# Idle products on TensorE taken out of the mixer stage of a two-layer encoder step

## What is computed

```python
p = rmsnorm(x, P['norm_mix']) @ P['w_in']
p_rg, p_gate, p_rw, p_mla = jnp.split(p, MIX_SPLITS, axis=-1)
y_rg, ... = rglru_mixer(p_rg, p_gate, rg_buf, rg_h, P)
y_rw, ... = rwkv7_mixer(p_rw, rw_shift, rw_state, P)      # delta-rule recurrence, 4 heads x 64
q_lat, q_rope, ckv, kr = mla_project(p_mla, pos, P)       # attention, 8 heads
y = jnp.concatenate([y_rg, y_rw, y_mla], axis=-1) @ P['w_out']
x = x + y
x = x + mem_attend(rmsnorm(x, P['norm_mem']), ...)
x = x + jnp.square(jax.nn.relu(rmsnorm(x, P['norm_ffn']) @ P['ffn_w1'])) @ P['ffn_w2']
```

## Time and profile before

| | us |
|---|---|
| median of 3 runs | 1875.14 (1874.27 to 1875.53) |
| the profiled execution | 1873.22 |
| its span in the trace | 1871.4 |
| TensorE matmul busy (records may overlap) | 1783.0, 95% |
| VectorE busy | 1143.1, 61% |
| ScalarE busy | 868.0, 46% |

### The profile page before, as it was taken

One profiled execution on the slowest core, in us unless ns is written; L12 is line 12 of the kernel. 1 busy time (PEld: TensorE's weight loads), 2 busy tenths in 40 slices (PEclk: granted clock), 3 DMA queues, 4 the chain that ended last, 5 costly groups with the idle time before them and its releaser, 6 DMA issues.

```text
span 1871.4 us, 38137 instructions
## 1 busy us (share of the span) xinstructions
PE 1783.0 (95%) x16290; PEld 1650.4 (88%) x16290; DVE 1143.1 (61%) x1977; ACT 868.0 (46%) x1588; POOL 259.5 (14%) x222
## 2 busy tenths in 40 slices
PE   5998988999999999999999999989999999999997
PEld 5985776899889999999999667769987999999996
DVE  6678666454457765666467776655444786556653
ACT  5444546453356544444345355554534664444432
POOL 2020000200013222221100100002000232222201
PEclk9999999999999999999999999999999999999998
DMA  6200001453012222222231000123610222222221
GB/s 225 68 20 1 4 3 48 147 172 133 35 57 80 102 95 99 91 91 95 88 127 57 9 1 4 37 94 122 214 57 13 101 79 102 93 95 96 91 92 59
DMA packets 38760, 149.56 MB, mean 80 GB/s; under 512 B 4416, under 2 KB 4576, under 8 KB 36928
## 3 DMA queue, kind: packets, MB, share of 16 engines
q1 hardware_dynamic: 36288, 131.05, 20.6%
q0 software_dynamic: 2304, 16.06, 2.3%
HBM read 139.68 MB, written 7.41 MB: 79 GB/s over the span
## 4 chain that ended last, share of the span: by engine, by line
PE 79%; DVE 10%; ACT 7%; issue 2%; POOL 1%; DMA 1%; DVEq 0%; ACTq 0%; SPq 0%; POOLq 0%
PE PS L816 58%; PE PS L979 13%; PE PS L1008 5%; PE PS L998 2%; DVE wL L1885 1%; DVE wL L1889 1%; ACT wH L1402 1%; DVE hbL L2358 1%; PE PS L1256 1%; ACT hb L1402 1%; ACT L1402 1%; DVE xT L1915 1%; DVE stat L2250 1%; POOL sq L707 1%; ACT sq L1402 0%
## 5 line engine op out<-in xcount | busy, mean ns | idle before, releaser
L1402 ACT ACTIVATE wH<-ring 128x1024 fp32r<-128x1024 f32 (+1 forms) x294 | 261.6, 891 | 327.6 <-PE PS L816 266.7
L816 PE MATMUL PS<-hH,wH 128*128 128x272 f32 x1760 | 384.4, 300 | 29.6 <-DVE hL L1898 19.0
L816 PE MATMUL PS<-hH,wL 128*128 128x272 f32 x1760 | 367.6, 290 | 0.0
L816 PE MATMUL PS<-hL,wH 128*128 128x272 f32 x1760 | 366.9, 290 | 0.0
L1889 DVE TENSOR_TENSOR wL<-ring,wH 128x1024 fp32r<-128x1024 f32 x182 | 230.9, 1270 | 188.1 <-ACT wH L1402 187.4
L816 PEld LDWEIGHTS PS<-hH,wH 128*128 128x128 f32 x1760 | 279.9, 190 | 46.1 <-issue 17.8
L816 PEld LDWEIGHTS PS<-hH,wL 128*128 128x128 f32 x1760 | 279.3, 190 | 0.0
L816 PEld LDWEIGHTS PS<-hL,wH 128*128 128x128 f32 x1760 | 277.9, 190 | 0.0
L979 PE MATMUL PS<-hbH,wH 128*128 128x272 f32 x784 | 227.1, 290 | 1.2 <-DVE hT L2414 0.9
L979 PE MATMUL PS<-hbH,wL 128*128 128x272 f32 x784 | 227.0, 290 | 0.0
L979 PE MATMUL PS<-hbL,wH 128*128 128x272 f32 x784 | 225.6, 288 | 0.0
(11 more groups left out here) (373 smaller groups left out, 3559.4 us busy)
## 6 DMA issues: line engine op xcount, KB each, us to landing
ring<-wall SPq DMA_DIRECT2D x238, 512.0 KB, 3.3
lw<-lw_in POOLq DMA_DIRECT2D x2, 1856.0 KB, 8.0
xT<-x_in SPq DMA_DIRECT2D x4, 544.0 KB, 5.9
y_out<-hT SPq DMA_DIRECT2D x8, 272.0 KB, 2.1
mem<-mem_in POOLq DMA_DIRECT2D x2, 1024.0 KB, 5.1
mks<-mks_in POOLq DMA_DIRECT2D x2, 1024.0 KB, 6.4
mvs<-mvs_in POOLq DMA_DIRECT2D x2, 1024.0 KB, 9.2
memk_out<-mkp POOLq DMA_DIRECT2D x2, 1024.0 KB, 6.1
```

What stands on the lines that cost most here:

```text
L816: return e.matmul(out, lhsT=a, rhs=b, start=start, stop=stop)
L1402: return e.activation(out, in_, f, **kw)
```

## The change

All calls of `keep_busy`, the function and its table are taken out. Nothing else changes: every other instruction keeps its place on its engine, and all waits stay.

```diff
-KEEP_BUSY = {0: 3, 2: 2, 3: 1, 4: 2}
 BESIDE_FACTORS = ("", "aaa", "aaa", "a", "a")
...
-                def keep_busy(n):
-
-                    for _ in range(n):
-                        mm(bank(7), ident, C("reset", 0, 512))
-
                 def recurrence():
                     for kind, g, b in REC_STEPS:
-                        if (kind, g) == ("score_m", NG - 1):
-                            keep_busy(2)
                         if kind == "tokens":
-                            if g == NG - 1:
-                                keep_busy(8)
                             tokens(g)
...
                 def attention():

-                    keep_busy(5)
                     e.wait_ge(s["cq_lo"], at(l, "cq_lo"))
                     for p in range(2):
                         project(p)
                         yield
                     for u, (h, b) in enumerate(UNITS):
-                        if u in KEEP_BUSY:
-                            keep_busy(KEEP_BUSY[u])
                         score(u)
```

## The result

| | before | after |
|---|---|---|
| median, us | 1875.34 (1874.27 to 1877.14, 4 runs) | 1892.16 (1886.74 to 1895.9, 4 runs) |
| profiled execution, us (its span) | 1873.22 (1871.4) | 1893.16 (1891.4) |

What follows compares the result with a forecast made beforehand. TensorE was taken to bound most of the kernel, VectorE and ScalarE the part ahead of the recurrence. The terms 0.5 + 0.25 - 0.95 + 0.5 + 0.4 + 0.87 gave +1.57 us a layer, +3.1 in all: 1878.2, range 1873.5 to 1883.0.

Steps and rivals of the forecast that it cites:

- The 18 products ahead of waits give nothing back: Products ahead of project(0), score(0), unit 2's wait and tokens(4): VectorE and ScalarE end those waits, so removal gains nothing.
- Rival C: Products ahead of waits were on the path after all; up to 32 us gained for both layers, 1843; chance 0.03.
- The five are worth 0.95 us a layer: Products between tokens(4) and merge(4): score_m starts 0.95 us earlier without them; bounds -4.4 and 0.
- The low clock at `project(0)`, `score(0)`: Start of the chain to tokens(4): matmuls slower after idling, +0.5 us for project(0) and +0.25 for score(0).
- rival A: The clock costs nothing on the path, only the gain of 0.95 us a layer is left; 1873.2; chance 0.12.
- `tokens(4)` to `score_m(4)`: Sign for the profile after: this stretch takes about 7.0 us instead of 7.5.
- From there to `merge(4)`: From score_m(4) on: +0.4 us for score_m at the low clock and what is left of it.
- I take one such stretch in each layer: After score_m: one further low-clock stretch of 3.4 us a layer, +0.87 us; bounds none and four.
- the quarter: Price of low clock: a 3.4 us stretch in layer 1 of the earlier trace cost 0.87 us, a quarter of its length.
- The bound of four stretches: Upper bound on further low-clock stretches of 3.4 us a layer after score_m; one was taken.
- The half of a throttled stretch by the Trainium skill: Skill page's cost rule for low-clock stretches: +5.5 us a layer, less 0.95, about +9 in all, 1884.
- Rival B: TensorE stays at 1.2 GHz through small products and becomes the bound; +7.2 us, 1882.3; sign: clock 0.50 beyond 173; chance 0.25.

Runs made afterwards that it cites:

- e1: Kernel before without the five products between tokens(4) and merge(4), the 18 ahead of waits kept; 1883.04 us, ratio 1.0042.
- e6: Kernel before without the three products ahead of the scores of units 3 and 4, the two ahead of score_m(4) kept; 1872.77 us, ratio 0.9988.
- e7: Kernel after with five products a layer put back ahead of the scores of unit 5, just behind the clock's fall; 1890.15 us, ratio 1.0073.
- e2: Kernel before without the 18 products ahead of waits, the five between tokens(4) and merge(4) kept; 1877.6 us, ratio 1.0021.
- e8: Kernel before plus three products of 256 columns a layer in waits 15 to 20 us behind tokens(4); 1874.71 us, ratio 0.9998.
- e11: Kernel before with only the two products a layer ahead of score_m(4) left; 1874.82 us, ratio 1.0004.
- e5: Kernel before without the two products ahead of score_m(4) in each layer, 21 left; 1872.75 us, ratio 0.999.
- e4: Kernel before with all 23 products a layer at their places, each 32 columns wide instead of 512; 1888.57 us, ratio 1.0072.

## Why the prediction was wrong

1. *The 18 products ahead of waits give nothing back*: right. In e1, where they stay, and in the kernel after, where they don't, VectorE and ScalarE end the same waits; `project(0)` comes 12.98 and 13.10 us into the stage. Rival C is out. What they do for the clock is another matter, see the end of 5.
2. *The five are worth 0.95 us a layer*: right in size, 0.80 in e6. But I costed them by what they hid behind only, and didn't ask what stands in their place. Their place is two waits, 1.37 us for ScalarE and 1.54 us for VectorE, between small matmuls, and there the clock falls (e1). The second counts more: with the first open and the second filled the clock held (e6), with the first short or gone and the second open it fell (e7).
3. *The low clock at `project(0)`, `score(0)`*: forecast +0.75, measured +0.85 and +0.70 in the kernel after and +1.05 in e2, where the clock was low throughout. Right for the sum, so rival A is out too. It is partly luck in layer 1: there `project(0)` alone cost 0.70 (1071.83 - 1066.30 = 5.53 us to `score(0)` for 4.83), and the clock was full again at `score(0)`.
4. *`tokens(4)` to `score_m(4)`*: forecast about 7.0 us, measured 168.72 - 161.62 = 7.10. Right. *From there to `merge(4)`*: forecast +0.4, measured 2.63 against 1.47, so +1.16: I had counted `score_m` itself, and not the transposes and scores behind it, which are as slow.
5. **The step that failed** is the last term: "I take one such stretch in each layer" at 0.87 us. It measured 5.4 and 13.0. Both of its factors were too small. The length behind `merge(4)` was 3.6 and 10.2 us in layer 0 and 37 in layer 1, not 3.4. The price was (169.26 - 155.3) / 37 = 0.38 us for each us at the low clock in layer 1, and (163.84 - 155.3) / 23.9 = 0.36 in layer 0 of e1 (whose `merge(4)` starts at 170.97, and whose stage takes 163.84 from there), not the quarter that the one short stretch of the earlier trace rows gave. But it isn't the length that sets the price, as stretches in other places show. First the stage of e8's layer 1 from `merge(4)` on and the stretch in it, then those of e11's layer 0:

```profile
1090.86:1247.64 156.78, 140.48 (x2584) 114.52 (x2583) 101.42 (x297) 87.14 (x235) 1.15 (x2) 0.99 0.05 17
1160.30:1163.60 3.30, 3.30 (x62) 3.18 (x60) 1.01 (x5) 0.00 (x0) 0.00 (x0) 0.50 0.02 5
...
173.44:329.54 156.10, 140.37 (x2577) 113.34 (x2577) 101.11 (x297) 86.47 (x234) 1.16 (x2) 0.98 0.05 17
322.80:329.54 6.74, 6.02 (x12) 2.98 (x11) 5.08 (x9) 5.17 (x7) 0.00 (x0) 0.50 0.21 78
```

Against the 155.3 of an undisturbed stage, 3.4 us in the one place cost 1.5 us (0.43 for each), 6.7 us in the other 0.8 (0.12). The bound of four stretches, 13.6 us, was drawn from nothing but that the trace of before had shown a single short one. It had shown the clock come back with the five products still in place, and so couldn't tell how long a stretch is without them. Length counts most: at the forecast's quarter the 37 us alone would have cost 9.5.

How the loss divides between the two groups of products is shown in part. Taking out the five alone costs 8.3 us (e1), the 18 alone 2.9 (e2), together 11.2 of the 16.8. The rest comes only with both gone, as in layer 1 of the kernel after, where the clock was low at `tokens(4)` and didn't come back for 47 us; but the runs of the kernel after spread by more than this rest.

6. The half of a throttled stretch by the Trainium skill (TensorE: Matmul & The Clock Gate, "HAM oscillation — how this bites in real kernels") is as far above the 0.36 to 0.38 of the long stretches as the quarter is below, and every stretch priced here cost less than half. Its estimate of 1884 is nearer to the result; both lie below it because of the lengths.
7. Rival B had the right mechanism, TensorE at 1.2 GHz through the small matmuls, and it was given one further stretch as well. "It decides as soon as the clock is not back by `merge(4)`" held in both layers, and the sign named for B came: in layer 0 the clock was 0.50 until 175.0, beyond 173. Its 1882.3 fell short by the same term.

What stays open: why the clock came back after 13 us in one layer and after 47 in the other of the same execution. The runs of the kernel after spread over 9 us, those of before beside them over 3 (over 8 in a set of 17), and nothing tried here tells what decides it. That products of 512 columns between `tokens(4)` and `score_m(4)` hold the clock was shown by adding and taking them away (e1, e5, e6 and e11), and that it takes their work by e4; that the waits as such are the trigger, the one of 1.54 us above all, is the reading of their place in time, since no run shortened them in another way.

## What to carry over

Before taking out work that "only" fills time, look at what the timeline has between its neighbours without it: here the harm started at the waits that opened, and the stage of small matmuls didn't get the clock back for up to 47 us. Put such filling into waits of TensorE and count it by the wait: here 1.88 us of it ahead of one wait was worth as much as 46 products, and the five of e7, in a place without a wait, set `merge(4)` back by 5.5 us. A price read from one disturbance holds for its place, and its length in a run that still has the remedy says nothing of the length without it.

## What the runs showed of the hardware

TensorE can be busy for 45.65 of 47.00 us with small matmuls and stay at 1.2 GHz throughout; so a high busy share of the profile doesn't bring the clock back. Long idling need not decide what comes later: behind 7.2 us without work the clock was back 3.1 us after `tokens(4)` in layer 0 of the kernel after (behind 7.9 us in its layer 1 it wasn't), and in e2 and e11 it was back in both layers within 6 us of `tokens(4)`, while in e1 it fell out of full clock at waits of 1.4 and 1.5 us. Products of 32 columns didn't hold the clock where products of 512 did (e4, 1888.57 us, against 1875). What a us at the low clock costs in this stage depends on where it lies, from 0.12 us (e11, layer 0) to 0.43 us (e8, layer 1).
